# FFN parts of three, four and four pairs instead of four, four and three, with the fourth pair in seven products

## The reference

```python
D_MODEL, SEQ, DEPTH, D_FF = 1024, 512, 2, 2816
def swiglu(h, w_gate, w_up, w_down):
    return (jax.nn.silu(h @ w_gate) * (h @ w_up)) @ w_down
for i in range(DEPTH):
    x = x + 0.5 * swiglu(rms_norm(x, ffn1_norm[i]), ffn1_w_gate[i], ffn1_w_up[i], ffn1_w_down[i])
    ...                     # token mixing, x = x + merged @ w_out[i]
    x = x + 0.5 * swiglu(rms_norm(x, ffn2_norm[i]), ffn2_w_gate[i], ffn2_w_up[i], ffn2_w_down[i])
return rms_norm(x, final_norm)
```

## Time and profile before

| | us |
|---|---|
| median of 3 runs | 2308.83 (2308.25 to 2308.97) |
| the profiled execution | 2309.07 |
| its span | 2307.3 |
| TensorE busy | 2292.3 |
| VectorE busy | 1492.6 |
| ScalarE busy | 838.5 |
| GpSimd busy | 27.7 |

### The profile page before, as it was taken

The page is one execution under the profiler, slowest core; times in us unless marked ns, Lnnn a source line. Parts: engine busy times, 40 slices in busy tenths (PEclk is TensorE's granted clock), DMA queues, the critical chain, the costliest instruction groups (busy, mean ns, idle before and its releaser), DMA issues.

```text
span 2307.3 us, 30268 instructions
## 1 busy us (share of the span) xinstructions
PE 2292.3 (99%) x13006; PEld 1992.2 (86%) x13006; DVE 1492.6 (65%) x1646; ACT 838.5 (36%) x899; POOL 27.7 (1%) x58
## 2 busy tenths in 40 slices
PE   8999999999999999999999999999999999999998
PEld 7899898887888888999988999989878888889997
DVE  6678687555544566877766877765554445669695
ACT  5333333323522333333433333432344223324332
POOL 4000000000000000000000000000000000000000
PEclk9999999999999999999999999999999999999999
DMA  5233224322222323232323232332212233232312
GB/s 158 81 109 115 87 92 132 92 73 64 73 87 86 122 93 97 92 127 82 102 92 109 92 129 73 109 115 83 83 51 78 87 115 108 91 110 92 125 59 91
DMA packets 231387, 222.59 MB, mean 96 GB/s; under 512 B 4208, under 2 KB 229600, under 8 KB 231264
## 3 DMA queue, kind: packets, MB, share of 16 engines
q1 hardware_dynamic: 225744, 215.29, 29.6%
q10 hardware_dynamic: 5520, 5.51, 0.7%
HBM read 218.69 MB, written 2.10 MB: 96 GB/s over the span
## 4 chain that ended last, share of the span: by engine, by line
PE 98%; DVE 1%; ACT 0%; DMA 0%; issue 0%; DVEq 0%; ACTq 0%
PE psum L557 60%; PE psum L603 14%; PE side L603 10%; PE psum L809 6%; PE psum L743 2%; PE side L827 1%; PE side L856 1%; PE side L557 1%; PE psum L569 1%; PE side L843 0%; PE side L838 0%; PE side L753 0%; PE side L725 0%; DMA x_in<-in_x_dram 0%; PE side L764 0%; PE psum L696 0%
## 5 line engine op out<-in xcount | busy, mean ns | idle before, releaser
L557 PE MATMUL psum<-h_hi,w_hi 128*128 128x512 f32 x1072 | 420.5, 392 | 1.0 <-DVE w_lo L1380 0.8
L557 PE MATMUL psum<-h_hi,w_lo 128*128 128x512 f32 x1072 | 417.3, 389 | 0.0
L557 PE MATMUL psum<-h_lo,w_hi 128*128 128x512 f32 x1072 | 417.1, 389 | 0.0
L1380 DVE TENSOR_TENSOR w_lo<-raw,w_hi 128x2048 fp32r<-128x2048 f32 (+2 forms) x135 | 275.5, 2041 | 107.9 <-ACT w_hi L932 107.3
L932 ACT ACTIVATE w_hi<-raw 128x2048 fp32r<-128x2048 f32 (+2 forms) x135 | 230.7, 1709 | 293.8 <-PE psum L557 270.4
L557 PE MATMUL psum<-act_hi,w_lo 128*128 128x512 f32 x656 | 255.2, 389 | 0.0
L603 PE MATMUL psum<-s_hi,hi 128*128 128x256 f32 x896 | 253.6, 283 | 0.0
L603 PE MATMUL psum<-s_lo,hi 128*128 128x256 f32 x896 | 253.6, 283 | 0.0
L557 PE MATMUL psum<-act_hi,w_hi 128*128 128x512 f32 x640 | 248.3, 389 | 0.0
L557 PEld LDWEIGHTS psum<-h_hi,w_hi 128*128 128x128 f32 x1072 | 201.3, 188 | 44.4 <-issue 2.5
L557 PEld LDWEIGHTS psum<-h_lo,w_hi 128*128 128x128 f32 x1072 | 201.3, 188 | 42.7 <-issue 1.4
(11 more groups left out here) (257 smaller groups left out, 4167.8 us busy)
## 6 DMA issues: line engine op xcount, KB each, us to landing
raw<-in_ffn_w_up_dram SPq DMA_DIRECT2D x44, 1024.0 KB, 5.3
raw<-in_ffn_w_gate_dram SPq DMA_DIRECT2D x43, 1024.0 KB, 5.4
raw<-in_w_in_dram SPq DMA_DIRECT2D x42, 1024.0 KB, 5.3
raw<-in_ffn_w_down_dram SPq DMA_DIRECT2D x32, 1024.0 KB, 5.3
raw<-in_ffn_w_down_dram SPq DMA_DIRECT2D x16, 768.0 KB, 5.8
raw<-in_w_in_dram SPq DMA_DIRECT2D x24, 512.0 KB, 4.0
raw<-in_w_out_dram SPq DMA_DIRECT2D x8, 1024.0 KB, 5.2
raw<-in_w_proj_b_dram SPq DMA_DIRECT2D x8, 512.0 KB, 3.4
```

The costliest lines, as they stand in the source:

```text
L557: mm = nc.tensor.matmul(dst[:, c * S:(c + 1) * S], l[:, a], r[:, b], start=first and k == ks[0] and n == 0, stop=last and k == ks[-1] and ...
L1380: nc.vector.tensor_tensor(w_lo[s][:, a], raw[s][:, a], w_hi[s][:, a].bitcast(F32), ALU.subtract).then_inc(split_made, 1)
```

## The change

The parts hold three, four and four pairs. The fourth pair thereby moves from part 0, where it was ordinary, into part 1, where it is made of seven products. The down units run over 6, 8 and 8 blocks. The units are now numbered: part 0 has 0 to 5 and down 6 to 9, part 1 has 10 to 17 and down 18 to 21, part 2 has 22 to 29 and down 30 to 33. What pair 3 did of the input blocks moves: one s_lo subtraction to behind pair 2, two to each of down units 0, 1 and 2 (s_ready is counted up in down unit 2 instead of 1); the last three s_hi roundings to down units 0 and 1. The split of the second down unit (unit 7), the first thing in the loop over d, keeps its place behind behind_pair(2). The activations' blocks are numbered within a part. The table free7, the side count that POOL waits for and the buffer of a part's first down unit (home_d) follow the new numbers; for the first down unit of part 2 the buffer is now chosen as in part 1.

```diff
-    DOWN_K = [(k, min(k + UNIT_K, KF)) for k in range(0, KF, UNIT_K)]
-    PART_PAIRS = ((0, 4), (4, 8), (8, 11))
-    PART_AT = (0, 12, 24)
-    FF_ALL = 34
+    PART_PAIRS = ((0, 3), (3, 7), (7, 11))
+    PART_AT = (0, 10, 22)
+    DOWN_K = [(2 * p0, 2 * p1) for p0, p1 in PART_PAIRS]
...
-        def home_d(b, d, w):
-
-            if d > 0:
-                return w, w_hi[w], w_lo[w]
-            return (w, hi_d, w_lo[w]) if b == 1 else (1 - w, hi_d, w_hi[w])
+        def home_d(d, w):
+
+            return w, w_hi[w] if d else hi_d, w_lo[w]
...
# SP: the table of what frees each buffer
-                free7 = {12: (done, 7), 13: (split_of, 11), 14: (split_of, 10), 15: (done, 12), 16: (done, 13), 17: (done, 14),
...
-                         29: (done, 26), 30: (done, 28), 31: (done, 27), 32: (done, 29), 33: (split_of, 30)}
+                free7 = {10: (done, 5), 11: (split_of, 9), 12: (split_of, 8), 13: (done, 10), 14: (done, 11), 15: (done, 12),
+                         16: (done, 13), 17: (done, 14), 18: (done, 15), 19: (done, 16), 20: (split_of, 18), 21: (done, 17),
+                         22: (split_of, 19), 23: (split_of, 21), 24: (split_of, 20), 25: (done, 22), 26: (done, 23),
+                         27: (done, 24), 28: (done, 25), 29: (done, 26), 30: (done, 27), 31: (done, 28), 32: (split_of, 30),
+                         33: (done, 29)}
...
# ScalarE
-                def inner(i, k_next=UNIT_K):
+                def inner(i):
...
-                    split(k_next)
+                    split(UNIT_K if i < PART_PAIRS[0][1] - 1 else DOWN_K[0][1])
...
                     if i == 2:
                         sums_hi(1, HI_ORDER[0:2])
-                    elif i == 3:
-                        sums_hi(3, HI_ORDER[4:6])
...
                     if i == 2:
                         sums_hi(2, HI_ORDER[2:4])
-                    elif i == 3:
-                        sums_hi(3, HI_ORDER[6:7])
...
                         if not end:
-                            split_d(b, k, d + 1) if b > 0 else split()
+                            split_d(k, d + 1) if b > 0 else split(k)
+                            if b == 0 and d < 2:
+                                sums_hi(3, HI_ORDER[4:6] if d == 0 else HI_ORDER[6:7])
...
# VectorE
-                    elif i == 3:
-                        sums_lo(HI_ORDER[0:2])
...
                     elif i == 2:
                         sums_b().then_inc(s_made, 1)
                         dve.wait_ge(s_made, layer * 6 + (3 if last else 0) + 3)
-                    elif i == 3:
-                        sums_lo(HI_ORDER[2:4])
+                        sums_lo(HI_ORDER[0:1])
...
                     if not first:
-                        split()
+                        split(UNIT_K if i < PART_PAIRS[0][1] - 1 else DOWN_K[0][1])
...
                         if not end:
-                            split_d(b, k, d + 1) if b > 0 else split()
+                            split_d(k, d + 1) if b > 0 else split(k)
...
-                        if b == 0 and d == 0:
-                            sums_lo(HI_ORDER[4:6])
-                        elif b == 0 and d == 1:
-                            sums_lo(HI_ORDER[6:7]).then_inc(s_ready, 1)
+                        if b == 0 and d < 2:
+                            sums_lo(HI_ORDER[1 + 2 * d:3 + 2 * d])
+                        elif b == 0 and d == 2:
+                            sums_lo(HI_ORDER[5:7]).then_inc(s_ready, 1)
```

More of the change, by code:

```diff
@@ L395, in done @@
                     sp.wait_ge(unit_done, g0 + n + 3)
-                free7 = {12: (done, 7), 13: (split_of, 11), 14: (split_of, 10), 15: (done, 12), 16: (done, 13), 17: (done, 14),
-                         18: (done, 15), 19: (done, 16), 20: (done, 17), 21: (done, 18), 22: (split_of, 20), 23: (done, 19),
-                         24: (split_of, 21), 25: (split_of, 23), 26: (split_of, 22), 27: (done, 24), 28: (done, 25),
-                         29: (done, 26), 30: (done, 28), 31: (done, 27), 32: (done, 29), 33: (split_of, 30)}
+                free7 = {10: (done, 5), 11: (split_of, 9), 12: (split_of, 8), 13: (done, 10), 14: (done, 11), 15: (done, 12),
[3 more added lines that the diff above has]
+                         33: (done, 29)}
                 for b, (p0, p1) in enumerate(PART_PAIRS):
@@ L426, in load_ffn @@
                         else:
-                            r = home_d(b, d, load.slot)[0]
+                            r = home_d(d, load.slot)[0]
                             dst = raw[r][:, 0:(k1 - k0) * UNIT_N].rearrange("p (k n) -> p k n", n=UNIT_N)
@@ L512, in _ @@
             for layer in range(DEPTH):
-                pool.wait_ge(side_evacuated[1], 4 + layer * 4 + (2 * layer + 1) * 7)
+                pool.wait_ge(side_evacuated[1], 4 + layer * 4 + (2 * layer + 1) * (PART_PAIRS[2][1] - PART_PAIRS[1][0]))
                 nc.gpsimd.affine_select(out=w_sT[:, :], in_=w_sT[:, :], compare_op=ALU.is_ge, fill=0.0, base=0,
@@ L657, in ffn @@
                         if d == 0 and b > 0:
-                            whi, wlo = home_d(b, d, s0)[1:]
+                            whi, wlo = home_d(d, s0)[1:]
                         ks = range(2 * (p1 - p0))
@@ L1011, in inner @@
                         sums_hi(1, HI_ORDER[0:2])
-                    elif i == 3:
-                        sums_hi(3, HI_ORDER[4:6])
                 def inner_hi(i):
                     act.wait_ge(act_made, counts["act"].next())
-                    nc.scalar.activation(pair(act_hi, i % 4), us[:, :], ACT.Copy).then_inc(act_hi_made, 1)
+                    nc.scalar.activation(pair(act_hi, i), us[:, :], ACT.Copy).then_inc(act_hi_made, 1)
                     if i == 2:
                         sums_hi(2, HI_ORDER[2:4])
-                    elif i == 3:
-                        sums_hi(3, HI_ORDER[6:7])
                 def done(n):
@@ L1050, in up_hi, with split_d @@
                     act.wait_ge(act_made, counts["act"].next())
-                    nc.scalar.activation(pair(act_hi, i % 4), us[:, :], ACT.Copy).then_inc(act_hi_made, 1)
-                def split_d(b, k, d):
-                    r, w, _ = home_d(b, d, slot[0])
+                    nc.scalar.activation(pair(act_hi, i), us[:, :], ACT.Copy).then_inc(act_hi_made, 1)
+                def split_d(k, d):
+                    r, w, _ = home_d(d, slot[0])
                     slot[0] = 1 - slot[0]
@@ L1085, in ffn @@
                             else:
-                                up_hi(p0 + (n - n0) // 2 - 1)
+                                up_hi((n - n0) // 2 - 1)
                             act.wait_ge(product_done, 6 * m + 1)
@@ L1093, in ffn @@
                             else:
-                                split_d(b, k, 0)
+                                split_d(k, 0)
                             if n < n0 + k - 2:
@@ L1100, in ffn @@
                             counts["unit"].next()
-                        up_hi(p1 - 1)
+                        up_hi(p1 - p0 - 1)
                     final = b == len(PART_PAIRS) - 1
@@ L1530, in behind_pair @@
                         dve.wait_ge(s_made, layer * 6 + (3 if last else 0) + 3)
-                    elif i == 3:
-                        sums_lo(HI_ORDER[2:4])
+                        sums_lo(HI_ORDER[0:1])
                 def act_lo_part(i):
                     dve.wait_ge(act_hi_made, counts["act_hi"].next())
-                    nc.vector.tensor_tensor(pair(act_lo, i % 4), us[:, :], pair(act_hi, i % 4).bitcast(F32),
+                    nc.vector.tensor_tensor(pair(act_lo, i), us[:, :], pair(act_hi, i).bitcast(F32),
                                             ALU.subtract).then_inc(act_ready, 1)
@@ L1589, in lo_rest, with split_d @@
                     nc.vector.tensor_tensor(blocks(w_lo_)[:, 1, :, 1, :], blocks(w_raw)[:, 1, :, 1, :], tile7(w, B22_).bitcast(F32), ALU.subtract).then_inc(split_made, 1)
-                def split_d(b, k, d):
-                    r, w, lo = home_d(b, d, slot[0])
+                def split_d(k, d):
+                    r, w, lo = home_d(d, slot[0])
                     slot[0] = 1 - slot[0]
@@ L1643, in ffn @@
                             unit7(b, n, n0, k, pending)
-                            pending = p0 + (n - n0) // 2 if n % 2 else None
-                        act_lo_part(p1 - 1)
+                            pending = (n - n0) // 2 if n % 2 else None
+                        act_lo_part(p1 - p0 - 1)
                     final = b == len(PART_PAIRS) - 1
```

## The result

The changed kernel takes 2313.89 us (median of 9 runs, 2313.41 to 2316.80) against 2308.95 (9 runs, 2308.25 to 2309.10): ratio 1.0026, 95% interval 1.0016 to 1.0035. It is slower by about 5 us (4.9), where I had forecast 3.2 (2312.0, range 2308.0 to 2315.0) and had called that too little to be told from no change; the interval leaves no change out.

A forecast was written before the change was run, and what follows sets the result against it. TensorE, busy 99% of the span, was taken to bound the kernel. From 2309.07 us, 6.4 removed and 9.6 of new waits gave 2312.3, or 2312.0 in terms of the median; range of 8 in 10: 2308.0 to 2315.0.

The forecast's parts named there:

- a further late link: Rival: VectorE's sets of units 8 and 9 slip, reaching TensorE in part 1; 2314.0 or 2316.0 us; 0.08 beyond 2313.4.
- What is removed: Fourth pair's two units per FFN, 48 long matmuls to 84 short: 0.80 us less each, 6.4 us over four FFNs.
- The wait at unit 7: Second down unit, each FFN: VectorE's split ends late, TensorE idles 2.33 us, 2.4 with slow first matmul; 9.6 us more.
- The slack of 0.85 us: Before the change, unit 7 due at 93.34 against its split's end at 92.34 plus 0.15 us.
- What moves along: Remaining s_lo and s_hi work goes into down units, hidden behind TensorE; loads land in time; no cost.
- The two full sets: VectorE's work from the takes of units 7 and 8: 8.0 us each against 8.16 us of TensorE, nobody waiting.
- The sum: Profiled execution 2309.07 - 6.4 + 9.6 = 2312.3 us; in terms of the runs' median, 2312.0 us, 0.14% longer.
- the clock falls in the new gaps: Rival at unit 7's gaps: each costs 2.2 us again, 8.8 in all, giving 2320.8 us; chance 0.06.
- gaps that bring the slow pace: Listed sign of being wrong: TensorE running at the slow pace after the gaps in the changed profile.
- the pace of 0.43: Slow matmul pace after a gap; the forecast expected first matmuls at 0.23, not 0.43.
- a gap of 0.76 us: TensorE's gap ahead of 25.26 us in the old profile, which did not bring back the slow pace.
- The outcome, slower by a little over 0.2%: Above 2313.4 us, chance 0.17: clock 0.06, further link 0.08, upper edge of the forecast 0.03.

The follow-up runs named there:

- the kernel with both splits first: Changed kernel with ScalarE and VectorE both splitting unit 7 ahead of s_hi, sums_b and s_lo of pair 2: 2302.35 us, ratio 0.9973 to the kernel before.

## Why the prediction was right, and where it fell short

The measured median lies in the range, and the parts of the sum hold. That it lies in the range is in part luck: the same kernel, timed again, had a median of 2315.35, beyond the upper end of 2315.0. The range reached up to 2315.0 for a further late link, which did not come; what filled it was the falling clock.

*What is removed.* Right. Six block, seven product and ordinary units keep their pitch, the weight subtraction has its 64 rows, and the kernel with both splits first gives the 6.4 us whole.

*The wait at unit 7.* Right in place, cause and size: 2.33 us forecast, 2.35 measured, with VectorE's split from 90.81 instead of 91.07 on a clock 0.26 us earlier. The slack of 0.85 us had been spent by the shorter unit alone; without the inserted s_lo there is still a wait of 1.2 us.

*What moves along.* Right. The s_lo cost nothing behind the split, s_ready and the first units of part 1 come in time, VectorE is 0.1 us behind the finished unit 9 and no more, and the loads are never waited for. The two full sets, forecast at 8.0 us each, lie between these rows and took 8.3 (0.43 of it idle) and 8.1:

```profile
101.16 1.23 DVE L1438 SCALAR_TENSOR_TENSOR xT<-psum,xT 128x1024 f32<-128x1024 f32 x1 [1.13 <-PE psum L555]
...
109.47 1.23 DVE L1438 SCALAR_TENSOR_TENSOR xT<-psum,xT 128x1024 f32<-128x1024 f32 x1
...
117.55 1.23 DVE L1438 SCALAR_TENSOR_TENSOR xT<-psum,xT 128x1024 f32<-128x1024 f32 x1
```

*The sum.* 2312.0 is what the kernel takes when the clock holds: 2312.15 and 2312.17 with the gap filled, 2312.4 in the best run of the changed kernel. The term that was missing is the one that I had put among the rivals with a chance of 0.06: "the clock falls in the new gaps". It falls behind two of the four in both profiles, and costs 1.5 to 1.6 us each time, not 2.2, so it adds 1.9 us to the first median (2313.89 against 2312.0) and 3.2 to the second (2315.35 against 2312.15), and not 8.8. So "gaps that bring the slow pace", which I had listed as a sign of being wrong, was seen, and so was the pace of 0.43 that I had said would not show. My fault was to treat it as a case that happens at all four gaps or at none. The rows bounded it badly: a gap of 0.76 us was harmless, the start of the run is slow from TensorE's first matmuls on (eight short ones in 1.94 us at 4.81, eight alike in 1.04 us at 14.29) and so doesn't show a clock falling in a gap, and the full clock in every slice that I counted against it could not have shown a spell. The gaps of 2.3 us should have carried a real chance of some spells. The outcome, slower by a little over 0.2% (0.26%), had 0.17. The Trainium skill (TensorE: Matmul & The Clock Gate, section "Why this matters for your kernels") warns of idle gaps between bursts; I had discounted it because these gaps are shorter than its figure. The runs agree with the warning and not with that bound: a start 2.35 us late (2.19 us idle) was enough in two of four places, one 3.5 us late in four of four.

## What to carry to other kernels

When a stage in whose shadow another engine prepares something gets shorter, add up that engine's queue from the moment the stage starts to the moment its next operand is ready, operation by operation. The order in the queues of VectorE and ScalarE was worth 13.0 us here (2315.35 against 2302.35 on the same chip; 3.2 of them are the spells), twice the 6.4 us of saved work, and the operand that is due next has to go first on both engines that make it. Price a new idle time of TensorE as the wait and a possible slow spell behind it, and keep its gaps below the size that the traces show to be harmless. If a late operand can't be helped, useless matmuls in the gap can still pay.

## What the runs showed of the hardware

- A gap of TensorE between two stretches of steady work, with a start 2.35 us late (2.19 us idle), was followed by about 3 us at 1.2 GHz in two of four places of each of two profiles, and that cost 1.5 to 1.6 us on top. The slow pace began 1.0 us after the work resumed (1234.8) or at once (2026.95). With starts 3.5 us late it happened in four of four places. With 1.28 us of idle time, and with starts 1.2 us late, it happened in no place of a profile, and the run times show no steps. Nothing between 1.28 and 2.19 us of idle time was run.
- The spells seem to split the times of one kernel into groups some 1.0 to 1.6 us apart (11 runs over 4.2 us); the kernels without spells stay within 1.9 us.
- Nine needless matmuls in each gap made the changed kernel 3.2 us faster on the same chip; with four it took 2312.17 us on the other chip, as much as with nine (2312.15).
